# One-core transformer kernel: another order of the SBUF buffers, dense operands at multiples of 128 bytes

## What is computed

```python
# first block
mod = silu(c) @ w_ada + b_ada                    # 2048 x 12288, one row
h = rmsnorm(x, norm1_g) * (1 + sc1) + sh1
proj = h @ w_in                                  # 2048 x 5456
o_sb = stick_breaking_attention(q_sb, k_sb, v_sb)
o_ds = dsa_attention(q_ds, k_ds, v_ds, q_ix, k_ix, w_ix * idx_scale)
x = x + g1 * (concat(rmsnorm(o_sb), rmsnorm(o_ds)) @ w_out)     # 2048 x 2048
h2 = rmsnorm(x, norm2_g) * (1 + sc2) + sh2
x = x + g2 * ((silu(gate) * val) @ w_down)       # gate, val: conv of h2 @ w_up (2048 x 11008); w_down 5504 x 2048
# second block, twice
proj = rms_norm(x, norm_g[l]) @ w_in[l]          # 2048 x 6726
q, kv = latent_q @ w_uq[l], latent_kv @ w_ukv[l] # 512 x 1152, 256 x 1536
x = x + concat(fox, mla, differential attention, gated) @ w_out[l]
return rms_norm(x, final_norm_g)
```

## Time and profile before

| | us |
|---|---|
| median of three runs | 2,141.72 |
| lowest of them | 2,128.18 |
| highest of them | 5,290.14 |
| span of the profiled execution | 2,133.0 |
| PE busy in it | 2,060.0 |
| DVE busy | 1,404.8 |
| ACT busy | 1,007.5 |
| POOL busy | 130.0 |

### The profile page before, as it was taken

One profiled execution on the slowest core, in us unless ns is written; L12 is line 12 of the kernel. 1 busy time (PEld: TensorE's weight loads), 2 busy tenths in 40 slices (PEclk: granted clock), 3 DMA queues, 4 the chain that ended last, 5 costly groups with the idle time before them and its releaser, 6 DMA issues.

```text
span 2133.0 us, 33911 instructions
## 1 busy us (share of the span) xinstructions
PE 2060.0 (97%) x13976; PEld 1865.6 (87%) x13976; DVE 1404.8 (66%) x2153; ACT 1007.5 (47%) x1490; POOL 130.0 (6%) x113
## 2 busy tenths in 40 slices
PE   5999999998999999999999999999999999999997
PEld 1679998787999999998888899999978999999876
DVE  2358999886667677666566676456566656565565
ACT  2234445534454454444545465344555545445454
POOL 0000000022000000000011011000001110000100
PEclk6999999999999999999999999999999999999999
DMA  9998798684777777656655546545545556545553
GB/s 362 383 359 308 239 393 324 216 312 148 232 236 235 227 242 262 190 157 244 192 178 199 178 153 198 200 142 161 176 158 182 171 161 205 172 158 171 166 178 119
DMA packets 267317, 462.97 MB, mean 217 GB/s; under 512 B 21526, under 2 KB 160028, under 8 KB 266652
## 3 DMA queue, kind: packets, MB, share of 16 engines
q1 hardware_dynamic: 265832, 459.66, 63.9%
q10 hardware_dynamic: 1332, 1.14, 0.2%
HBM read 458.62 MB, written 2.13 MB: 216 GB/s over the span
## 4 chain that ended last, share of the span: by engine, by line
PE 84%; DVE 7%; DMA 3%; ACT 2%; issue 2%; ACTq 1%; POOL 0%; SPq 0%; DVEq 0%
PE PS L312 36%; PE PS L311 20%; PE PS L1359 7%; PE PS L1364 7%; PE PS L1360 7%; DVE WLO L302 2%; PE PS L1202 2%; ACT WHI L294 1%; DMA BIG<-w_ada 1%; PE PS L413 1%; DMA X<-x 1%; PE PS L1216 1%; DVE WK L1041 1%; DVE BIG L1687 1%; PE PS L1031 0%
## 5 line engine op out<-in xcount | busy, mean ns | idle before, releaser
L302 DVE TENSOR_TENSOR WLO<-RAWT,WHI 128x1024 fp32r<-128x1024 f32 (+7 forms) x694 | 830.3, 1203 | 405.6 <-ACT WHI L294 404.7
L294 ACT ACTIVATE WHI<-RAWT 128x1024 fp32r<-128x1024 f32 (+7 forms) x694 | 694.0, 1015 | 358.4 <-PE PS L1364 198.9
L312 PE MATMUL PS<-WHI,HH 128*128 128x512 f32 (+5 forms) x1304 | 507.3, 389 | 17.9 <-DVE HLO L789 7.3
L312 PE MATMUL PS<-WHI,HLO 128*128 128x512 f32 (+5 forms) x1304 | 497.8, 382 | 0.0
L312 PE MATMUL PS<-WLO,HH 128*128 128x512 f32 (+5 forms) x1304 | 340.7, 383 | 0.8 <-DVE WLO L302 0.8
L1359 PE MATMUL PS<-HH,WHI 128*128 128x256 f32 x1376 | 328.6, 280 | 7.1 <-POOL HLO L1050 7.1
L1360 PE MATMUL PS<-HLO,WHI 128*128 128x256 f32 x1376 | 327.3, 279 | 0.0
L311 PE MATMUL PS<-HH,WHI 128*128 128x256 f32 x1280 | 311.8, 285 | 0.0
L312 PEld LDWEIGHTS PS<-WHI,HH 128*128 128x128 f32 x1304 | 246.2, 189 | 66.7 <-DVE HLO L789 14.6
L311 PE MATMUL PS<-HLO,WHI 128*128 128x256 f32 x1280 | 303.1, 278 | 0.0
L312 PEld LDWEIGHTS PS<-WLO,HH 128*128 128x128 f32 x1304 | 245.6, 189 | 43.2 <-DVE WLO L302 1.6
(11 more groups left out here) (301 smaller groups left out, 1614.0 us busy)
## 6 DMA issues: line engine op xcount, KB each, us to landing
RAWT<-w_in SPq DMA_DIRECT2D x96, 1024.0 KB, 5.2
RAWT<-w_up SPq DMA_DIRECT2D x168, 512.0 KB, 4.9
AD<-w_ada SPq DMA_DIRECT2D x152, 512.0 KB, 6.3
RAWT<-w_out SPq DMA_DIRECT2D x96, 512.0 KB, 4.9
RAWT<-w_down SPq DMA_DIRECT2D x86, 512.0 KB, 4.6
BIG<-w_ada SPq DMA_DIRECT2D x40, 512.0 KB, 12.2
RAWT<-w_in SPq DMA_DIRECT2D x16, 832.0 KB, 4.5
RAWT<-w_in SPq DMA_DIRECT2D x16, 512.0 KB, 4.6
```

The costliest lines, as they stand in the source:

```text
L294: act.activation(WHI[:, (q % HL) * GR:(q % HL) * GR + size], r, ACT.Copy).then_inc(S("hi_done"), 1)
L302: dve.tensor_tensor(WLO[:, (q % HL) * GR:(q % HL) * GR + size], r, h.bitcast(F32), ALU.subtract)\
L312: pe.matmul(o, feat, weight, start=start, stop=stop)
```

## The change

Only where buffers lie is changed. RAWT, WHI, WLO, AD, WK and KX are allocated ahead of BIG and not behind it, and the two ranges of the latents move up by 16 columns (64 bytes).

```diff
-LATENT, KVB = (3152, 9872), W2 - 1536
+LATENT, KVB = (3168, 9888), W2 - 1536
@@
         HH, HLO = sb("HH", 2 * D, F32R), sb("HLO", 2 * D, F32R)
+        RAWT = sb("RAWT", RAW * 2 * GR)
+        WHI, WLO = sb("WHI", HL * GR, F32R), sb("WLO", HL * GR, F32R)
+        AD = sb("AD", 5 * 1024)
+        WK = sb("WK", 3072)
+        KX = sb("KX", 256)
         with nc.sbuf_tensor("BELOW", [P, LATENT[0]], F32), nc.sbuf_tensor("LATHI", [P, 1536], F32R) as LATHI, \
                 nc.sbuf_tensor("BETWEEN", [P, LATENT[1] - LATENT[0] - 1536], F32), \
                 nc.sbuf_tensor("LATLO", [P, 1536], F32R) as LATLO:
             pass
         BIG = sb("BIG", 2 * W2)
-        RAWT = sb("RAWT", RAW * 2 * GR)
-        WHI, WLO = sb("WHI", HL * GR, F32R), sb("WLO", HL * GR, F32R)
-        AD = sb("AD", 5 * 1024)
-        WK = sb("WK", 3072)
-        KX = sb("KX", 256)
         CST = sb("CST", C_W)
```

## The result

The changed kernel takes 2,159.1 us (median of four runs, 2,155.95 to 2,161.39) against 2,128.2, 2,131.1 and 2,141.7 us of the kernel before beside it (a fourth run, disturbed, took 5,290 us and enters no ratio). The ratio is 1.0126, 95% interval 1.0109 to 1.0143: slower by 1.3%, where 2,086 us, 46.5 less than the profiled 2,133, had been forecast. The profiled execution spans 2,159.5 us, 26.5 more than that of before.

A forecast was written before the change was run, and what follows sets the result against it. TensorE's dense matmuls were taken to bound the kernel, wholly after about 470 us. Gains 29.4 + 3.5 + 5.1 + 1.5 + 7 = 46.5 us take 2,133.0 to 2,086; own range 2,070 to 2,105, with rivals 2,045 to 2,125.

The forecast's parts named there:

- What bounds the kernel: TensorE's dense matmuls: a cheaper matmul counts wholly after about 470 us, little before 200 us, partly between.
- The row on which the forecast rests: Stationary WHI or WLO: moved HH, beginning at a multiple of 128, said to be 2 to 6 ns cheaper than LATHI.
- Moved WHI and WLO: 512-column matmuls of line 312 and others: 2,208 after 480 us, each 13.3 ns cheaper, 29.4 us, between 11 and 35.
- The lower bound of 5 ns: Least gain per 512-column matmul, to 224.4 ns, taken from the slower moved HH at 11 ns over its column time.
- The rival that the surplus is not the start's: The 13 to 16 ns are a fixed fp32r price: 2,130, chance 0.1; weaker form, 512 columns partly gain: 2,113, chance 0.15.
- The smaller terms: Gains besides the two main forms: w_out 3.5 us, 416 columns 5.1 us, the latents with their 384 columns 1.5 us.
- Moved HH and HLO: 256 columns in w_up and line 311, some 7,200 after 470 us: settling in the better pace, 0 to 13 us, 7 taken.
- the first rival: Both operands matter: a misplaced stationary start costs while a matmul streams; 256 columns fall to 109.5 ns, total 2,050, chance 0.2.
- The rival called Slower: Both operands starting at multiples of 128 make reads collide: 13.3 ns on some 12,000 matmuls, total 2,250, chance 0.04.
- the turning point of 3.3 ns: In Slower, the loss per matmul from which the change's sign turns: 40 us won over 12,000 matmuls.
- The rule of 16-byte lines: Skill page's SBUF lines of 16 bytes: 48 and 64 are both multiples, so by that page alone the change gives nothing.

The follow-up runs named there:

- Experiment 2: Bare fp32r matmuls without the model, a hundred pairs of stationary and moved starts: no 256-column pace below 113.3 ns, 512 columns between 226.6 and 236.5.
- experiments 1 and 3: 1: changed kernel, WHI and WLO 64 bytes on: 2,123.8 us, ratio 0.9951. 3: kernel before, HH, HLO and SPARE 64 bytes on: 2,160.1 us, ratio 1.0133.
- experiments 6 and 7: 6: changed kernel, WHI, WLO 76 bytes past features modulo 256, latents moved to match: 2,119.8 us. 7: also w_down, w_out_2 features 196 bytes on: 2,118.8 us.

## Why the prediction was wrong

**What bounds the kernel** was right. TensorE sets the time from about 470 us on, and what its matmuls lost there (25.3 us net) passed to the span almost whole (23.7). Nothing moved before 130 us, and VectorE, ScalarE and the transfers took no part. Line 397 kept 1.84 us with AD aligned too, and 388 columns gained nothing.

**The row on which the forecast rests failed.** "A moved operand that begins at a multiple is cheaper" compared LATHI (119.7) with HH (113.8 and 117.5), which in the kernel before differ in two things: where they begin, and how far they lie from the stationary operand. The first was taken. Experiment 2 shows that between these starts (multiples of 64) it costs nothing and that the second is the whole difference. The wrong addresses (48 for 64) hid that LATHI and WHI began alike, which was the hint.

**Moved WHI and WLO, 29.4 us of the sum,** measured 2.2 ns a matmul in w_down and 1.8 on the mean, in place of 13.3: 3.9 us. The 13 ns above one column per cycle were read as one more piece of 128 bytes, because 128 bytes are 32 columns. But with all starts at 128 it is still 227.2 - 213.3 = 13.9, and 120.0 - 106.7 = 13.3 at 256 columns. The lower bound of 5 ns, from the moved HH, fell with the same step. The rival that the surplus is not the start's was nearer for this form (0.1 and 0.15). The smaller terms failed with it: w_out gave 24.84 - 24.60 = 0.2 us for 3.5, 416 columns (188.3 and 188.8 ns) nothing for 5.1, and the latents some 0.2 for 1.5, with 384 columns on them slower (173.3 to 4.22 / 24 = 175.8 ns).

**Moved HH and HLO, 7 us of the sum,** had the wrong sign: 29 us lost. It was supposed that two streams that step through the same 128 bytes settle in the better pace. They settle in a worse one, 120.0, in every stretch. Here rows 8 were asked for what they cannot tell. Line 397 moves two columns, so hardly a second stream reads beside its loads, as the first rival already said of it; that caution was not applied to the sum.

**The rival called Slower** had the mechanism in kind: two operands that begin alike disturb each other, with the two paces of one form as the sign for it. It was given 0.04, on nothing but rows 8. Its price was off: 4.1 ns on 7,100 matmuls of one form, where 13.3 ns on 12,000 had been written, and the turning point of 3.3 ns was set against a gain of 40 us that did not exist.

**The rule of 16-byte lines** (the Trainium skill, SBUF — State Buffer, Specifications) would have given no change. For the common start of both operands the runs agree with it at multiples of 32 (119.8 to 120.0 ns) and not at odd multiples of 16 (116.6 and 118.2), and for their distance they disagree (120.0 at 0, 113.3 at 64). The same skill's statement that the loads have a read port of their own and do not steal from the running matmul (TensorE: Matmul & The Clock Gate, Step-by-step: what each phase is for) is not what these runs show for fp32r, whatever the ports: with everything else equal, the load's address moves the pace of 256 columns between 113.3 and 123.5 ns.

**What stays open:** whether and in which unit the two reads meet, and why the period is 256 bytes; what the starts modulo 32 do beside the distance; why some distances (52, 64, 96, 168) have two or three settled paces; why 512 columns at 180 and at 120 have 229.3 and 229.0 ns in the kernel and 234.0 and 226.6 bare; and the 4 to 5 us by which experiments 1 and 3 are early at 130 us. That the scatter of the kernel before (2,128 to 2,141 us) comes from how often it settles at 117.8 is argued from the 4.5 ns between its paces, not shown.

## What to carry to other kernels

When the same form of instruction has two prices in one trace, list everything that differs between the two places, the operands' positions to each other too, before one of them becomes a cause; and read addresses from the built program. A row stands for another only where the same things run beside it: a row with nothing in its moved stream cannot clear a rival about two streams. Where fp32r matmuls load weights each time and move 256 columns that begin at a multiple of 128 bytes, put the weight buffers 76 bytes (modulo 256) past the features and not at the same alignment. Here that was worth 0.6% against the kernel before, and some 1.8% against the tidy layout (medians of 2,119.8 and 2,159.1 us, not measured side by side).

## What the runs showed of the hardware

- An fp32r matmul of 256 columns with its own weight load runs at 113.3 to 123.5 ns, depending first on the stationary start minus the moved start modulo 256 bytes. It never reached the 106.7 ns of one column per cycle, in 64 distances.
- At multiples of 32 the common start of both operands does not matter: 119.8 to 120.0 ns at 0, 32, 64, 96, 128 and 192. At odd multiples of 16 it does: 116.6 ns at 16, 118.2 at 48, 80 and 112.
- At a distance of 64 bytes the pace settles at 117.8 or 113.3 ns in the first few matmuls of a stretch and stays there until other matmuls interrupt it (before: at 711 and 888 us); at 76 it settled at 113.3 to 113.8 in all four stretches and all through `w_up`.
- With 512 columns bare matmuls run at 226.6 to 242.1 ns and w_down in the kernels here at 227.2 to 233.8. The two agree at the distances 0, 128 and 192 with both starts at multiples of 64, and not in experiments 6 and 7, where the moved weights begin 12 bytes past a multiple of 32.
